# Dense layer: the block sums of a seven-product matrix scheme on VectorE in place of GpSimd

## What is computed

```python
h = rmsnorm(x, norm_mix[0]);  x = x + pool_mixer(h, pool_w[0], pool_scale[0])
h = rmsnorm(x, norm_ffn[0]);  x = x + swiglu(h, ffn_wg[0], ffn_wu[0], ffn_wd[0])

def swiglu(h, wg, wu, wd):             # wg, wu: 1024 x 3584, wd: 3584 x 1024
    return (jax.nn.silu(h @ wg) * (h @ wu)) @ wd
```

## Time and profile before

| | us |
|---|---|
| median of 3 runs | 4070.25 (4065.38 to 4071.65) |
| profiled execution, its time / its span | 4066.12 / 4063.5 |
| TensorE busy | 3868.9, 95% |
| VectorE busy | 2529.3, 62% |
| ScalarE busy | 1665.3, 41% |
| GpSimd busy | 663.5, 16% |
| pooling mixer, until TensorE's first transpose of the dense layer | 0 to 76.4 |
| dense layer: rows and tile 0; tiles 1 to 27; down product | 76.4 to 125.5; to 666; to 936 |

### The profile page before, as it was taken

One profiled execution on the slowest core, in us unless ns is written; L12 is line 12 of the kernel. 1 busy time (PEld: TensorE's weight loads), 2 busy tenths in 40 slices (PEclk: granted clock), 3 DMA queues, 4 the chain that ended last, 5 costly groups with the idle time before them and its releaser, 6 DMA issues.

```text
span 4063.5 us, 62129 instructions
## 1 busy us (share of the span) xinstructions
PE 3868.9 (95%) x22510; PEld 3369.3 (83%) x22510; DVE 2529.3 (62%) x3837; ACT 1665.3 (41%) x2459; POOL 663.5 (16%) x626
## 2 busy tenths in 40 slices
PE   8999999998998899888899999999999999999998
PEld 6777777886887566667899999999999999999987
DVE  6777776454434777645455555555666666666678
ACT  4322223332333777751323323333344444444455
POOL 3323232001230344424100100000010101001010
...
DMA packets 181531, 633.88 MB, mean 156 GB/s; under 512 B 28734, under 2 KB 56894, under 8 KB 144705
## 3 DMA queue, kind: packets, MB, share of 16 engines
...
## 4 chain that ended last, share of the span: by engine, by line
PE 50%; DVE 1%; DMA 0%; issue 0%; ACT 0%; POOL 0%; DVEq 0%; POOLq 0%; SPq 0%; ACTq 0%
PE moe_ps L425 11%; PE moe_ps L427 11%; PE moe_ps L426 10%; PE moe_ps L467 6%; PE moe_ps L468 6%; PE moe_ps L469 6%; PE moe_ps L406 1%; PE moe_ps L434 0%; PE moe_ps L435 0%; PE moe_ps L438 0%; DMA moe_wd_raw<-in_moe_wd 0%; DVE moe_yacc L353 0%; DMA moe_stage<-h_moe,moe_ids 0%; DVE moe_gu_lo L317 0%; DVE moe_ht_lo L313 0%
## 5 line engine op out<-in xcount | busy, mean ns | idle before, releaser
L425 PE MATMUL moe_ps<-moe_ht_hi,moe_gu_hi 128*128 128x256 f32 (+4 forms) x3136 | 936.6, 299 | 1.5 <-DVE moe_ht_lo L313 1.5
L427 PE MATMUL moe_ps<-moe_ht_hi,moe_gu_lo 128*128 128x256 f32 (+4 forms) x3136 | 936.1, 298 | 0.0
L426 PE MATMUL moe_ps<-moe_ht_lo,moe_gu_hi 128*128 128x256 f32 (+4 forms) x3136 | 935.6, 298 | 0.0
L234 ACT CAST moe_gu_hi<-moe_gu_raw 128x2048 fp32r<-128x2048 f32 x226 | 430.9, 1907 | 508.8 <-PE moe_ps L427 490.4
L317 DVE TENSOR_TENSOR moe_gu_lo<-moe_gu_raw,moe_gu_hi 128x2048 fp32r<-128x2048 f32 x226 | 517.5, 2290 | 171.6 <-ACT moe_gu_hi L234 171.6
L425 PEld LDWEIGHTS moe_ps<-moe_ht_hi,moe_gu_hi 128*128 128x128 f32 x3136 | 596.2, 190 | 5.2 <-issue 1.7
L426 PEld LDWEIGHTS moe_ps<-moe_ht_lo,moe_gu_hi 128*128 128x128 f32 x3136 | 597.0, 190 | 3.5
L427 PEld LDWEIGHTS moe_ps<-moe_ht_hi,moe_gu_lo 128*128 128x128 f32 x3136 | 596.0, 190 | 0.0
L353 DVE SCALAR_TENSOR_TENSOR moe_yacc<-moe_ps,job_weights,moe_yacc 128x512 f32<-128x512 f32 x504 | 374.9, 750 | 326.9 <-PE moe_ps L469 326.9
L467 PE MATMUL moe_ps<-moe_wd_hi,moe_hid_hi 128*128 128x512 f32 x1008 | 395.9, 393 | 0.0
L468 PE MATMUL moe_ps<-moe_wd_lo,moe_hid_hi 128*128 128x512 f32 x1008 | 393.4, 390 | 0.0
...
## 6 DMA issues: line engine op xcount, KB each, us to landing
moe_gu_raw<-in_moe_wgu SPq DMA_DIRECT2D x228, 1024.0 KB, 4.8
moe_wd_raw<-in_moe_wd SPq DMA_DIRECT2D x112, 1024.0 KB, 6.6
...
first_sum<-in_ffn_wgu SPq DMA_DIRECT2D x14, 1024.0 KB, 5.0
shared<-in_ffn_wgu SPq DMA_DIRECT2D x14, 1024.0 KB, 6.5
h_rows<-in_ffn_wd SPq DMA_DIRECT2D x14, 1024.0 KB, 10.7
wd_parts<-h_rows SPq DMA_DIRECT2D x14, 1024.0 KB, 8.7
hid_parts<-h_rows SPq DMA_DIRECT2D x14, 1024.0 KB, 4.1
```

Of the source, the lines that this page charges most:

```text
L234: act.copy(gu_hi[s][:, :, :, :].rearrange("p a k c -> p (a k c)"), gu_raw[r][:, :]).then_inc(s_gu_hi, 1)
L425: pe.matmul(out[:, 0:W], gu_hi[s][:, half, k, :], ht_hi[:, k, 0:W], start=(k == 0), stop=False)
L426: pe.matmul(out[:, 0:W], gu_hi[s][:, half, k, :], ht_lo[:, k, 0:W], start=False, stop=False)
L427: last = pe.matmul(out[:, 0:W], gu_lo[s][:, half, k, :], ht_hi[:, k, 0:W], start=False, stop=(k == KT - 1))
```

## The change

- **Row parts.** T1 to T4 (parts 5, 6, 7, 4) are made by VectorE in the pooling mixer, in buffers of their own (`h_parts`), from the rows of tiles i and i+4: four operations each behind `normed_mid` of tiles 4 to 7.
- **Down and hidden sums.** VectorE makes them: `side_sum(j, n)`, four in each tile. Odd tiles sum the down weights of their pair, even tiles from 2 on the hidden blocks of the pair before; the last pair's follow the last tile. Sum 0 stands at the end of the tile before, sum 1 ahead of `take_p7`, sums 2 and 3 behind the low part 7.
- **Order.** Turns and products of tile 0 go in the order of all tiles, a product behind each turn. The third and fourth weight sums now stand ahead of the low part 6, the low part 2 behind the side sums, the low part 3 ahead of `last_hidden` (and on ScalarE the high part 3 ahead of the second Silu). `first_hidden`'s wait for the stored pair is as before.
- **End of the tiles.** SyncE stores the last down sums behind the loads of chunks 0 to 3, and not ahead of them.
- **Memory.** The dense layer's buffers are laid out anew, so that high parts 2, 4, 3 and low part 3 take the place of `h_parts`.

```diff
@@ pool_mixer, VectorE
+            def row_parts(i):
+                first, second = h_rows[:, i, 0:D // 2], h_rows[:, i, D // 2:D]
+                late_first, late_second = h_rows[:, i + 4, 0:D // 2], h_rows[:, i + 4, D // 2:D]
+                t1, t2, t3, t4 = (h_parts[p][:, i, :] for p in (5, 6, 7, 4))
+                dve.wait_ge(s_hf, i + 5)
+                dve.tensor_tensor(t1, late_first, first, ALU.subtract).then_inc(s_parts, 1)
+                dve.tensor_tensor(t3, late_second, late_first, ALU.subtract).then_inc(s_parts, 1)
+                dve.wait_ge(s_parts, 4 * i + 1)
+                dve.tensor_tensor(t2, late_second, t1, ALU.subtract).then_inc(s_parts, 1)
+                dve.wait_ge(s_parts, 4 * i + 3)
+                dve.tensor_tensor(t4, second, t2, ALU.subtract).then_inc(s_parts, 1)
@@ loop over tiles
                 if i:
                     normed_mid(i - 1)
+                if i >= 5:
+                    row_parts(i - 5)
             normed_mid(TILES - 1)
+            row_parts(3)
@@ dense_ffn, SyncE
-                if j % 2:
+                if j % 2 and j + 1 < MT:
                     store_down_sums(j // 2)
-                    if j // 2 + 1 < PAIRS:
-                        load_down(j // 2 + 1)
+                    load_down(j // 2 + 1)
             for x in range(4):
                 load_chunk(x)
+            store_down_sums(PAIRS - 1)
             store_hidden(PAIRS - 1)
@@ GpSimd
-            for n, (p, a, b, turned) in enumerate(((5, 7, 1, 0), (7, 3, 7, None), (6, 3, 5, 1), (4, 2, 6, 2))):
-                for i in range(4):
...
-                    combine(row_part(p, i), row_part(a, i), row_part(b, i), ALU.subtract, s_made)
...
-            for q in range(PAIRS):
-                down_sums(q)
-                hidden_sums(q)
@@ VectorE
+            def down_sum(q, n):
+                dve.wait_ge(s_wd_loaded, 16 * (q + 1))
+                if q:
+                    dve.wait_ge(s_wd_out, 16 * q)
...
+                to, of, less = ((t1, b12, b11), (t2, b22, t1), (t3, b22, b12), (t4, b21, t2))[n]
+                dve.tensor_tensor(to, of, less, ALU.subtract).then_inc(s_wd_sum, 1)
+            def hidden_sum(q, n):
+                if n == 0 and q:
+                    pair_stored(dve, q - 1)
+                if n == 0:
+                    dve.wait_ge(s_hid_2, 2 * q + 2)
...
+                dve.tensor_tensor(to, a, b, ALU.add if n == 0 else ALU.subtract).then_inc(s_hid_sum, 1)
+            def side_sum(j, n):
+                if j % 2:
+                    down_sum(j // 2, n)
+                elif j:
+                    hidden_sum(j // 2 - 1, n)
@@ VectorE, tile j
                 if more:
+                    sums(j + 1, (3,))
                     weights_lo(j + 1, 6)
-                    sums(j + 1, (3,))
                     weights_lo(j + 1, 5)
+                side_sum(j, 1)
                 take_p7(j)
                 take_p5(j)
                 if more:
                     weights_lo(j + 1, 7)
-                    weights_lo(j + 1, 2)
...
+                side_sum(j, 2)
+                side_sum(j, 3)
+                if more:
+                    weights_lo(j + 1, 2)
                 take_p4(j)
                 first_hidden(j)
...
                 take_p3(j)
+                if more:
+                    weights_lo(j + 1, 3)
                 last_hidden(j)
                 if more:
-                    weights_lo(j + 1, 3)
+                    side_sum(j + 1, 0)
+            for n in range(4):
+                hidden_sum(PAIRS - 1, n)
@@ TensorE
             turn(0)
-            turn(1)
-            product(0, 1)
...
+            for kind in range(1, 7):
+                turn(kind)
+                product(0, ORDER[kind - 1])
+            product(0, 3)
```

More of the change, by code:

```diff
@@ L576, in pool_mixer @@
         s_mid_out = [sem(f"mid_out{s}") for s in range(3)]
-        s_half, s_seen, s_pool, s_scaled = (sem(n) for n in ("half", "seen", "chain", "scaled"))
+        s_half, s_seen, s_pool, s_scaled, s_parts = (sem(n) for n in ("half", "seen", "chain", "scaled", "parts"))
         s_sq_x, s_rs_x, s_xh, s_d, s_diff, s_y, s_mid, s_sq_mid, s_rs_mid, s_hf = (
@@ L830, in row_part @@
         def row_part(p, i):
-            tile, at = {1: (0, 0), 3: (4, W), 2: (0, W), 5: (0, 0), 7: (4, 0), 6: (4, W), 4: (0, W)}[p]
+            if p in h_parts:
+                return h_parts[p][:, i, :]
+            tile, at = {1: (0, 0), 2: (0, W), 3: (4, W)}[p]
             return h_rows[:, tile + i, at:at + W]
         def units():
-            return [(u, TURNED[u // 4], u % 4) for u in range(28)]
+            return [(u, ORDER[u // 4], u % 4) for u in range(28)]
         def turn_bank(u):
@@ L1057, in _ @@
                 last_gate(j)
-                if more:
-                    weights_hi(j + 1, 3)
             for x in range(2, CHUNKS):
@@ L1163, in _ @@
             weights_lo(0, 1)
-            rows_lo(1)
-            sums(0, (1,))
-            rows_lo(2)
-            weights_lo(0, 5)
-            rows_lo(3)
-            sums(0, (3,))
-            weights_lo(0, 6)
-            rows_lo(4)
-            rows_lo(5)
-            weights_lo(0, 2)
-            weights_lo(0, 7)
-            weights_lo(0, 4)
-            take_p6(0)
-            rows_lo(6)
-            weights_lo(0, 3)
+            sums(0, (1, 3))
+            for kind in range(1, 7):
+                rows_lo(kind)
+                weights_lo(0, ORDER[kind])
+                if kind == 3:
+                    take_p6(0)
             for j in range(MT):
@@ L1265, in _ @@
             turn(0)
-            turn(1)
-            product(0, 1)
-            turn(2)
-            turn(3)
-            product(0, 5)
-            turn(4)
-            turn(5)
-            product(0, 6)
-            turn(6)
-            for p in (2, 7, 4, 3):
-                product(0, p)
+            for kind in range(1, 7):
+                turn(kind)
+                product(0, ORDER[kind - 1])
+            product(0, 3)
             for j in range(1, MT):
-                for p in REST:
+                for p in ORDER:
                     product(j, p)
```

103 lines of the change are left out of this document (38 added, 65 removed).

## The result

| | before | changed |
|---|---|---|
| median of the first comparison, us | 4067.82 (4 runs, 4064.48 to 4071.65) | 4032.11 (4 runs, 4029.70 to 4033.74) |
| ratio, 95% interval | | 0.9911 (0.9894 to 0.9929) |
| profiled execution, time / span, us | 4066.12 / 4063.5 | 4029.7 / 4027.9 |
| TensorE's first transpose | 76.40 | 80.31 |
| marker of tile 0, counted from it | 49.35 | 44.29 |

Two later comparisons of the same two kernels gave 4036.24 against 4067.88 (0.9926, 0.9912 to 0.9940) and 4035.14 against 4068.73 (0.9917, 0.9903 to 0.9930): 32 to 36 us in all three.

The account below looks back on a forecast made before the run. TensorE, busy 95% of the span, was taken as the bound, so time comes only from its waits. Terms 3.9 - 4.7 - 26.4 - 2.3 = -29.5 us from the median 4070.25 gave 4041 us, range 4032 to 4051.

Parts of the forecast that it names:

- mixer: End of the pooling mixer: VectorE's 16 added row-part operations start the dense layer later, at 80.3 us, +3.9 us.
- tile 0: First dense tile: without GpSimd's row parts and with new order, its marker (start of `take_p3`) comes sooner, -4.7 us.
- gate/up tiles: Dense layer's tiles: TensorE's waits for `take_p6` and `take_p7` in even tiles go, 26 steps to 19.04, -26.4 us.
- down product, chunk 4: Start of the down product: chunk 4's load comes sooner, so TensorE's 2.35 us wait goes, -2.3 us.
- Which of the two facts is the cause: Even tiles: GpSimd's sums, not the buffer, make VectorE's operations with two SBUF operands slow, 1.75 against 0.69 us.
- The store's stall: Even tiles, `first_hidden`: VectorE waits 1.3 us for the hidden sums' store, 13 times, costing nothing up to about 6.0 us landing.
- the marker would step 19.04 in every tile: Gate/up tiles: the start of `take_p3`, once per tile, was to step by 19.04 us in every tile.
- All later stages are behind a barrier and shift unchanged: Stages behind the dense layer: they only shift with its end, with no term of their own in the sum.
- Rival 1: Mixer and tile 0 both at their bad bounds (5 and 0): -23.7 us, 4046.5 us; chance 0.12.
- Rival 2: `first_hidden` in even tiles: the hidden sums' store lands late, at 9.7 us giving +18.6, 4089 us; chance 0.05.
- Rival 3: Even tiles: VectorE is slow for a reason of its own, the odd buffer; 4113 us; chance 0.03.
- Rival 4: Gate/up tiles: the wait only moves, VectorE's order leaving 1 us a tile in all 27; 4068 us; chance 0.04.

Follow-up runs that it names:

- pool_two: Changed kernel plus twelve unused GpSimd additions of 128x340, two SBUF inputs, per pair of tiles; median 4041.26 us, 0.9932 of before.
- late_store: Changed kernel with an extra 1 MB store queued ahead of the store of the hidden sums; median 4043.30 us, 0.9937 of before.
- old_order: Changed kernel, sums on VectorE, with the low part 3 swap and the weight sums' place undone; median 4034.94 us, 0.9926 of before.

## Why the forecast was right and wrong

The sum, term by term, in us:

| term | forecast | first profile |
|---|---|---|
| mixer | +3.9 | +3.91 (76.40 to 80.31) |
| tile 0 | -4.7 | -5.06 (49.35 to 44.29) |
| gate/up tiles | -26.4 | -26.3 (540.45 to 514.1, marker of tile 0 to the first down product) |
| down product, chunk 4 | -2.3 | -2.7 (269.2 to 266.5) |
| dense layer | -29.5 | -30.2 |
| behind it | 0 | -5.4 |

- **Mixer: right, to the step.** The four groups of row parts stand where they were walked: 0.69 us are left of the idle 3.35, tile 7's first step waits from 66.48 to 69.13 (walked 69.0), the last normed rows start at 75.38 (75.15), the last row part ends at 79.3 (79.0). TensorE began 1.0 us behind it and not 1.25, so the two small errors cancel.
- **Tile 0: right, as far as one profile of before tells** (49.35; it took 52.13 in another, which would make the term -7.8). `take_p7` at 35.9 us from the first transpose (36.1), product 4 at 36.75 (36.9), the clock at 0.50 behind the wait.
- **Gate/up tiles: the size right, the cause incomplete.** The sentence "Which of the two facts is the cause" took GpSimd's hold on VectorE for the whole of it. That hold is real (0.69 against 1.75 us, and pool_two), and removing it is enough. But it is not needed: the swap of the low part 3, which the forecast walked only together with the move of the sums, brings 20.3 us by itself with GpSimd as busy as ever. The forecast had not walked the new order against the old load. Had it done so, the 0.70 us of idle time and the 1.78 of the first weight sum stood in the trace.
- **The store's stall: right.** 13 waits of 1.5 us (forecast 1.3), landing in 4.1, no effect on TensorE. The statement that the marker would step 19.04 in every tile was wrong in form: 19.7 and 18.4 in turn, 38.08 a pair.
- **Chunk 4: right**, no wait is left in the down product; the 0.4 more were not followed up.
- **The total: 8.9 us too high.** The step that failed is "All later stages are behind a barrier and shift unchanged": the term behind the layer was put at nothing, and the only scatter allowed for was the 6 us of the three whole runs. The stages do shift, but the stretch to the experts takes 1000.5 to 1017.4 us from one profile to the next, and the one profile that stood for before had 1008.3, the changed one 1002.3. That is 5.4 us (from the layer's end to the end of the span); 0.7 lie in the dense layer; 2.4 in the base, since a fourth run of the kernel before brought its median to 4067.82 where 4070.25 had been shown; the last 0.4 are rounding and what a median leaves over against one profile. By the two later comparisons the miss is 4.8 and 5.9, so the size of the miss is in part luck of the draw.
- **Rivals.** None came. Rival 1: mixer and tile 0 stood at the walk. Rival 2: its mechanism is confirmed by late_store, with TensorE waiting from a landing of 6.1 to 6.4 us on, for the forecast's 6.0; the store just doesn't land late (4.1 us, as before). Rival 3: the sums on `shared` take 685 ns in even tiles. Rival 4: no wait moved; old_order shows that even the stall for the Silu is covered.
